# Hyena's engine order woven anew, and the odd filter spectra's sums formed in the attention stage

## The chip, the cores and the metric

One core of a Trainium2 chip runs the whole program. The metric is the device time in microseconds; lower is better. The engines are TensorE (PE, matrix products into PSUM), VectorE (DVE), ScalarE (ACT), GpSimd (POOL, which doesn't reach PSUM) and SyncE (SP, which here issues the weight loads). Each runs its own instruction stream in order and waits on counting semaphores.

## The reference

Two layers of a hybrid backbone run over 128 context and 512 latent tokens of width 1024. What bears on the change is the Hyena branch, `y = x0 * (h (*) (x1 * u) + bias * (x1 * u))`:

```python
def bidir_long_conv(u, h, bias):
    L, C = u.shape[1], u.shape[2]
    g = jnp.concatenate([h[:, 0], jnp.zeros((1, C), jnp.float32), h[:0:-1, 1]], axis=0)
    U = jnp.fft.rfft(u, n=2 * L, axis=1)
    G = jnp.fft.rfft(g, n=2 * L, axis=0)
    y = jnp.fft.irfft(U * G[None], n=2 * L, axis=1)[:, :L]
    return y + u * bias
```

`h` comes from a small sine MLP of the positions (`hyena_filters`), once per layer. Beside it a windowed attention runs on the same input projection. Each branch is projected, gated and merged, then comes a gated feed-forward part. The modulation of both groups of tokens is `silu(cond) @ w_ada + b_ada`.

## The kernel before

Features lie on the 128 partitions, the tokens of both groups along the row. Every f32 operand of a large product is split into a high and a low part (ACT writes `hi`, DVE writes `lo` = source - `hi`), and a product is three matmuls. Weights arrive in chunks of up to 1 MB in two raw buffers. SP issues them in the fixed order of `stream()`, and before item n it waits for the consumer of item n-2, so a load can't overtake the one ahead of it. Each chunk is split by `split(g)` on ACT and on DVE into one of two slots; a slot is free when the product of two chunks earlier has been made (`chunk_done`).

The Fourier transforms are matmuls with cosine and sine matrices, in five "pairs" of spectrum rows: pair 0 for the context, pairs 1 and 2 for the even frequencies of the latent tokens, pairs 3 and 4 for two parts of the odd ones.

**Prologue.** PE forms the filter rows of both layers (`filter_rows`, L545), DVE multiplies them by the window and forms sums and differences, five steps a layer (`filter_blocks`, L1559 to L1583), PE turns them into spectra (`g_spectrum`, L563), and ACT (later DVE) copies those out. POOL stores them to a DRAM buffer `g_kept` (`g_spill`). Before that `g_combine` (L2146, L2149) forms the sum and the difference of the odd pairs 3 and 4. In between, the first modulation vectors are made: chunks (0, 4) and (0, 5) of `w_ada` by PE (`ada`, L525), chunks (0, 6) and (0, 7) by DVE (`ada_t`, L1525). The stream's order is (0, 6), (0, 4), (0, 7), (0, 5), then the layer's weights. In the second layer's filter blocks `ada_t(0, 6)` stands behind step 1.

**Attention.** Five blocks; two tiles of the Hyena projection (z) lie beside each on PE. POOL is nearly idle.

**Hyena.** After the last block PE transposes u (`u_transposed`), then makes the last z tile, spectra 0 to 2 of u (`spectrum`, L797), four rows of the attention's projection (`attn_projected`, L781, which reads the chunk gA), the context's inverse (L942), spectra 3 and 4, and the latent inverses of pairs 1 to 4 (`inverse`, L819). The inverses read chunk gI, which lies in the slot of gA. DVE forms the complex products with the kept filter spectra (L1887 to L1905 for pairs 0 to 2, L1920 to L1939 for 3 and 4, which first add and subtract the two parts) and their low halves `y_lo` (L1631), and splits the chunks gA, gF1, gI and gG between them (L1618). ACT makes the high halves `y_hi`. Pairs 1 and 3, and 0, 2 and 4, share a slot of `y_hi` and `y_lo`. When the last `y_lo` is ready, POOL clears pads of `h_src_rows`, and ACT and DVE form the rows for the gates, of which PE's next tile takes one after the other (`both`, L691).

## Time and profile before

| | us |
|---|---|
| median of 3 runs (lowest, highest) | 2029.27 (2028.94, 2031.91) |
| profiled execution: time | 2029.84 |
| its span, first to last instruction | 2026.9 |
| PE busy | 1963.9 |
| DVE busy | 1168.8 |
| ACT busy | 740.6 |
| POOL busy | 195.6 |

Times in the views count from the span's start. The prologue lasts to about 97, the attention and Hyena stages of layer 0 to about 367, those of layer 1 from about 1060 to 1327. In a timeline row the number in brackets is the time that the engine stood idle before it, and what ended that. `x4` after the shapes is the number of instructions merged into the row.

### The profile page before, as it was taken

The page shows a single profiled execution, that of the slowest core. Times are in us where ns is not written, and L with a number is a line of the kernel's source. Part 1 is how long each engine was busy: PE and PEld are TensorE (multiplying, and loading weights), DVE is VectorE, ACT ScalarE, POOL GpSimd, SP SyncE. Part 2 cuts the span into 40 slices and gives each one's busy share as a digit, 9 for nine tenths or more (in the row PEclk, how much of TensorE's full clock was granted, in tenths as well). Part 3 has the DMA queues.
Part 4 walks back from the last instruction along what each step waited for, and adds up shares of the span by engine and source line. Part 5 has one row for each costly group of instructions (what it writes and reads, how often), then busy time and mean ns, then how long its engine had stood idle before and what let it go on. Part 6 is the DMA issues. An engine that isn't in the chain of part 4 may idle for free.

```text
span 2026.9 us, 30168 instructions
## 1 busy us (share of the span) xinstructions
PE 1963.9 (97%) x12914; PEld 1881.4 (93%) x12914; DVE 1168.8 (58%) x1743; ACT 740.6 (37%) x1098; POOL 195.6 (10%) x210
## 2 busy tenths in 40 slices
PE   8899998999999999999999999899999999999997
PEld 3599997999999999999989999899998999999996
DVE  7824559787477677767455456953347343243435
ACT  3534444422273321333244445532227332133313
POOL 0320001100150000000121000110015000000011
PEclk9999999999999999999999999899999999999999
DMA  8431012255213335443322101212221211221121
GB/s 329 154 116 66 16 56 99 99 189 185 85 63 128 143 141 196 153 166 120 106 73 100 48 27 61 84 60 92 78 79 63 84 63 65 91 84 63 64 72 53
DMA packets 37438, 203.39 MB, mean 100 GB/s; under 512 B 4294, under 2 KB 7927, under 8 KB 19256
## 3 DMA queue, kind: packets, MB, share of 16 engines
q1 hardware_dynamic: 30904, 181.37, 25.1%
q0 software_dynamic: 3312, 13.35, 1.9%
q10 hardware_dynamic: 3088, 6.75, 0.9%
q8 instruction: 101, 1.65, 0.3%
q14 instruction: 33, 0.27, 0.0%
HBM read 193.31 MB, written 8.14 MB: 99 GB/s over the span
## 4 chain that ended last, share of the span: by engine, by line
PE 83%; DVE 10%; ACT 4%; issue 2%; ACTq 0%; DMA 0%; POOL 0%; SPq 0%; DVEq 0%
PE gemm_psum L618 51%; PE gemm_psum L648 15%; PE gemm_psum L671 3%; PE gemm_psum L631 3%; PE aux_psum L758 2%; PE gemm_psum L691 2%; PE aux_psum L739 2%; PE aux_psum L747 1%; ACT h_src_rows L1186 1%; PE gemm_psum L525 1%; DVE aux_psum L1793 1%; PE gemm_psum L563 1%; DVE w_lo L1618 1%; DVE x L1797 1%; PE aux_psum L545 1%
## 5 line engine op out<-in xcount | busy, mean ns | idle before, releaser
L618 PE MATMUL gemm_psum<-h_hi,w_hi 128*128 128x322 f32 x2144 | 497.1, 313 | 0.3
L618 PE MATMUL gemm_psum<-h_hi,w_lo 128*128 128x322 f32 x2144 | 493.5, 311 | 0.0
L618 PE MATMUL gemm_psum<-h_lo,w_hi 128*128 128x322 f32 x2144 | 491.3, 310 | 0.0
L618 PEld LDWEIGHTS gemm_psum<-h_hi,w_hi 128*128 128x128 f32 x2144 | 362.8, 189 | 4.4 <-issue 3.1
L618 PEld LDWEIGHTS gemm_psum<-h_lo,w_hi 128*128 128x128 f32 x2144 | 362.1, 189 | 0.0
L618 PEld LDWEIGHTS gemm_psum<-h_hi,w_lo 128*128 128x128 f32 x2144 | 361.9, 189 | 0.0
L1618 DVE TENSOR_TENSOR w_lo<-w_raw,w_hi 128x2048 fp32r<-128x2048 f32 (+4 forms) x128 | 244.6, 1911 | 182.1 <-ACT w_hi L1116 181.1
L1116 ACT ACTIVATE w_hi<-w_raw 128x2048 fp32r<-128x2048 f32 (+4 forms) x128 | 204.1, 1594 | 170.7 <-PE gemm_psum L648 65.6
L1525 DVE CUSTOM_DVE_ANT_0 aux_psum<-w_raw,cond_by_row 128x1024 f32<-128x1024 f32 x160 | 191.0, 1257 | 5.0 <-DMA w_raw<-in_ada_t 4.7
L1751 DVE SCALAR_TENSOR_TENSOR x<-gemm_psum,mod,x 128x128 f32<-128x128 f32 (+2 forms) x144 | 55.4, 434 | 158.7 <-PE gemm_psum L648 128.9
L648 PE MATMUL gemm_psum<-act_hi,w_lo 128*128 128x322 f32 x616 | 141.9, 312 | 0.0
L648 PE MATMUL gemm_psum<-act_lo,w_hi 128*128 128x322 f32 x616 | 141.6, 311 | 0.0
L648 PE MATMUL gemm_psum<-act_hi,w_hi 128*128 128x322 f32 x616 | 141.5, 311 | 0.0
L1653 DVE SCALAR_TENSOR_TENSOR gate_acc<-gate_rows,par,gate_acc 128x642 f32<-128x642 f32 x88 | 80.2, 912 | 75.8 <-ACT gate_acc L1194 74.3
L1824 DVE TENSOR_TENSOR gate_acc<-gate_acc,gemm_psum 128x644 f32<-128x644 f32 x40 | 33.0, 826 | 143.7 <-PE gemm_psum L618 143.7
L648 PEld LDWEIGHTS gemm_psum<-act_hi,w_hi 128*128 128x128 f32 x616 | 104.3, 189 | 0.0
L648 PEld LDWEIGHTS gemm_psum<-act_hi,w_lo 128*128 128x128 f32 x616 | 104.2, 189 | 0.0
L648 PEld LDWEIGHTS gemm_psum<-act_lo,w_hi 128*128 128x128 f32 x616 | 103.9, 189 | 0.0
L1135 ACT ACTIVATE act_hi<-gate_acc 128x644 fp32r<-128x644 f32 x44 | 32.7, 742 | 153.5 <-DVE gate_acc L1824 147.1
L1193 ACT ACTIVATE gate_rows<-gemm_psum 128x644 f32<-128x644 f32 (+1 forms) x48 | 31.8, 662 | 144.4 <-PE gemm_psum L618 140.0
L2159 POOL TENSOR_TENSOR sums<-x 128x644 f32<-128x644 f32 x4 | 6.4, 1589 | 790.5 <-DVE x L1751 790.5
L671 PE MATMUL gemm_psum<-h_hi,w_hi 128*128 128x322 f32 x224 | 72.2, 323 | 10.3 <-POOL h_lo L2127 3.8
(349 smaller groups left out, 3264.5 us busy)
## 6 DMA issues: line engine op xcount, KB each, us to landing
w_raw<-in_w_up SPq DMA_DIRECT2D x44, 1024.0 KB, 4.8
w_raw<-in_ada_t SPq DMA_DIRECT2D x42, 1024.0 KB, 4.7
w_raw<-in_w_down SPq DMA_DIRECT2D x32, 704.0 KB, 4.1
w_raw<-in_w_gate SPq DMA_DIRECT2D x16, 1024.0 KB, 4.8
w_raw<-in_w_z SPq DMA_DIRECT2D x12, 1024.0 KB, 4.7
w_raw<-in_w_out SPq DMA_DIRECT2D x8, 1024.0 KB, 4.7
ada_early<-in_ada SPq DMA_DIRECT2D x4, 1024.0 KB, 19.4
g_kept<-g_rows_out POOLq DMA_DIRECT2D x8, 512.0 KB, 4.4
```

Of the source, the lines that this page charges most:

```text
L618: last = mm(gp[:, 2 * (t % 2) + hf, 0:HALF], w[:, off + P * kk:off + P * (kk + 1)], moving(kk, lo)[:, hf * HALF:(hf + 1) * HALF], start=kk ...
L631: last = mm(gp[:, 2 * (t % 2) + hf, 0:HALF], w[:, off + P * kk:off + P * (kk + 1)], moving(kk, lo)[:, half(hf)], start=kk == 0 and n == 0, ...
L648: last = mm(gp[:, 2 * (t % 2) + hf, 0:HALF], w[:, off + P * kk:off + P * (kk + 1)], moving(kk, lo)[:, half(hf)], start=kk == 0 and n == 0, ...
L671: last = mm(banks(c, p_, hf), w[:, P * (KD * c + kk):P * (KD * c + kk + 1)], (hlo if lo else hhi)[:, kk, half(hf)], start=kk == 0 and n == ...
L691: last = mm(gp[:, 2 * ((t0 + c) % 2) + hf, 0:HALF], w[:, P * (KD * c + kk):P * (KD * c + kk + 1)], moving(kk, lo)[:, hf * HALF:(hf + 1) * ...
L739: last = mm(ax[:, n % 4, at:at + P * m], q[pr, j, tok(b)], rhs, start=True, stop=True)
L758: last = mm(ax[:, 2, HD * n:HD * (n + 1)], p_t(n)[:, P * kb:P * (kb + 1)], v[:, HD * (n % 2):HD * (n % 2 + 1)], start=kb == 0, stop=kb == ...
L1116: run(whi[s][:, 0:n], raw[st_ % 2][:, 0:n], ACT.Copy).then_inc(sem["w_hi"], raised("w_hi"))
L1525: V.tensor_tensor_reduce(out=ada_out[:, :] if first else ax[:, 2 * gr:2 * gr + 2, :].rearrange("p a b -> p (a b)"), in0=raw[n % 2][:, D_MO ...
L1618: TT(wlo[s][:, 0:n], raw[STEP[(lane.layer, "g", g)] % 2][:, 0:n], f32(whi[s][:, 0:n]), ALU.subtract).then_inc(sem["w_split"], raised("w_sp ...
L1653: STT(acc[:, 1:ROW - 1], z[:, a:a + ROW - 2], w(tap), acc[:, 1:ROW - 1], ALU.mult, ALU.add).then_inc(sem[event if tap else "dve_order"], r ...
L1751: STT(x[:, m, a:b], gp[:, 2 * (t % 2) + h, a - HALF * h:b - HALF * h], mod[:, gate + m, gr:gr + 1], x[:, m, a:b], ALU.mult, ALU.add)\
```

## The change

- In the prologue `g_combine` is gone: all five pairs of both layers are stored as they come, and layer 1's four last stores stand between rows of `h_lo`. `ada_t(0, 6)` moves from behind step 1 to behind step 3.
- In each layer's attention stage POOL reads pairs 3 and 4 back into a new tile `g_parts` (in space that Hyena's `early` and `u_fold` use later), forms the sum and the difference in four operations and stores them over the old ones. DVE waits for these stores before it writes `u_fold`.
- In Hyena PE's order becomes: spectrum 0, last z tile, spectra 1 and 2, rows 0 and 1 of the projection, context inverse, row 2, spectra 3 and 4, row 3, inverses. The PSUM banks of the spectra and of row 2 move to suit.
- DVE's order becomes: products of pair 0 at once, then the u halves, gA's split, the x0 taps, low halves of pair 0, gF1's split, and so on; gI's split moves behind the first odd product, and the context's result ahead of the products of pair 2.
- The copies of one partition (`us[0:1]` from `prod[0:1]`) move from DVE to ACT. ACT makes the high halves of u's odd blocks (`u_hi(5, 9)`) later, and gI's split follows row 3 of the projection.

The diff, without the list of semaphores and with context lines cut (eight spaces of indentation taken off):

```diff
@@ -310,6 +310,8 @@
         ufold = sb("u_fold", [P, 4, HY_W], F32, s3)
+    with ExitStack() as s3:
+        g_parts = sb("g_odd_parts", [P, 5, HY_W], F32, s3)
     early = sb("attn_projected", [P, EARLY, ROW], F32, s2)
@@ -346,7 +348,6 @@
     feat = sb("feat", [FEAT, NT], F32, s2)
-g_first = sb("g_first_half", [P, 2, HY_W], F32, s)
 dreg = sb("d_block", [P, 2, HY_W], F32, s)
@@ -369,7 +370,7 @@
     ot_bank = lambda b: gp[:, 2, :] if b + 1 < NB else ax[:, 2, :]
-    spec_bank = lambda r: ax[:, r, :] if r < 2 else gp[:, r % 4, :]
+    spec_bank = lambda r: ax[:, r, :] if r < 2 else gp[:, (r - 2) % 4, :]
     ROPE_ORDER = [4, 0, 1, 2, 3]
@@ -430,7 +431,7 @@
     G_SLOT = [0, 1, 2, 0, 1]
-    EARLY_BANKS = [(1, 2), (1, 0), (1, 2), (1, 0)]
+    EARLY_BANKS = [(1, 2), (1, 0), (1, 0), (1, 0)]
@@ -911,29 +912,27 @@
     to_features(NB - 1)
-    pe.wait_ge(sem["at_lo"], due("at_lo", NB - 1))
-    tile(9, 1, KD, KD * P, h_mov, "z_mm")
-
     pe.wait_ge(sem["us_ready"], due("us_ready", 1))
...
     spectrum(0, U_V[0])
+    pe.wait_ge(sem["at_lo"], due("at_lo", NB - 1))
+    tile(9, 1, KD, KD * P, h_mov, "z_mm")
+
+    pe.wait_ge(sem["us_ready"], due("us_ready", 3))
+    spectrum(1, U_V[1])
     pe.wait_ge(sem["z_acc"], due("z_acc", 12))
-    for p_ in range(1, 3):
-        pe.wait_ge(sem["us_ready"], due("us_ready", 1 + 2 * p_))
-        spectrum(p_, U_V[p_])
+    pe.wait_ge(sem["us_ready"], due("us_ready", 5))
+    spectrum(2, U_V[2])
     pe.wait_ge(sem["w_split"], due("w_split", gA + 1))
...
     attn_projected(1)
-    for n in (2, 3):
-        pe.wait_ge(sem["pa_out"], due("pa_out", n - 1))
-        attn_projected(n)
...
     pe.wait_ge(sem["y_ready"], due("y_ready", 2))
-    pe.wait_ge(sem["pa_out"], due("pa_out", 3))
+    pe.wait_ge(sem["pa_out"], due("pa_out", 1))
     s = slot_of(gF1)
@@ -942,9 +941,13 @@
     last.then_inc(sem["cinv_mm"], raised("cinv_mm"))
+    pe.wait_ge(sem["pa_out"], due("pa_out", 2))
+    attn_projected(2)
     pe.wait_ge(sem["us_rest"], due("us_rest", 4))
...
     spectrum(4, U_V[4])
+    pe.wait_ge(sem["pa_out"], due("pa_out", 3))
+    attn_projected(3)
     pe.wait_ge(sem["w_split"], due("w_split", gI + 1))
@@ -1314,35 +1317,41 @@
     split(gA)
-    u_hi(5, 9)
...
+    def y_high(p_):
+
+        for o in range(2):
+            src = us[:, o, :] if p_ < 3 else (us, prod)[o][:, p_ - 3, :]
+            if p_ < 2:
+                act.wait_ge(sem["y_src"], due("y_src", 2 * p_ + o + 1))
+                run(us[0:1, o, :], prod[0:1, 1 - o, :], ACT.Copy).then_inc(sem["act_order"], raised("act_order"))
+                act.wait_ge(sem["act_order"], now("act_order"))
+            hi(yhi[:, Y_SLOT[p_], 1 - o, :], src, "y_src", 2 * p_ + o + 1, "y_hi")
+
     act.wait_ge(sem["usp_mm"], due("usp_mm", 4))
+    y_high(0)
     split(gF1)
-    for p_ in range(PAIRS):
-        for o in range(2):
-            if p_ == 2:
-                act.wait_ge(sem["cinv_mm"], due("cinv_mm", 1))
-            if p_ >= 3:
-                act.wait_ge(sem["linv_mm"], due("linv_mm", p_ - 2))
-            src = us[:, o, :] if p_ < 3 else (us, prod)[o][:, p_ - 3, :]
-            hi(yhi[:, Y_SLOT[p_], 1 - o, :], src, "y_src", 2 * p_ + o + 1, "y_hi")
-        if p_ == 0:
-            early_row(0)
-            early_row(1)
-        if p_ == 1:
-            early_row(2)
-            early_row(3)
-            split(gI)
-        if p_ == 2:
-            for o in range(2):
-                act.wait_ge(sem["usp_mm"], due("usp_mm", 7 + o))
-                run(ureg[:, 2 * o, :], spec_bank(6 + o), ACT.Copy).then_inc(sem["odd_out"], raised("odd_out"))
-            split(gG)
+    u_hi(5, 9)
+    early_row(0)
+    early_row(1)
+    y_high(1)
+    early_row(2)
+    for o in range(2):
+        act.wait_ge(sem["usp_mm"], due("usp_mm", 7 + o))
+        run(ureg[:, 2 * o, :], spec_bank(6 + o), ACT.Copy).then_inc(sem["odd_out"], raised("odd_out"))
+    act.wait_ge(sem["cinv_mm"], due("cinv_mm", 1))
+    y_high(2)
+    early_row(3)
+    split(gI)
+    split(gG)
+    for p_ in (3, 4):
+        act.wait_ge(sem["linv_mm"], due("linv_mm", p_ - 2))
+        y_high(p_)
     act.wait_ge(sem["usp_mm"], due("usp_mm", 10))
@@ -1569,7 +1578,7 @@
         TT(dreg[:, m % 2, :], fprod[:, 0, :], fprod[:, 1, :], ALU.subtract).then_inc(sem["gs_src"], 1)
-        if l and m == 1:
+        if l and m == 3:
             dve.wait_ge(sem["cond_rows"], 1)
@@ -1869,50 +1878,53 @@
     dve.wait_ge(sem["ut_out"], due("ut_out", 5))
+    dve.wait_ge(sem["g_kept_odd"], 48 * (L + 1))
     for n in range(4):
...
     u_lo(1, 3)
-    x0_tap(1, 0)
-    u_lo(3, 5)
-    x0_tap(1, 2)
-    split(gA)
-    for p_ in range(3):
+
+    def products(p_):
...
         ur, ui = spec_bank(2 * p_), spec_bank(2 * p_ + 1)
-        dve.wait_ge(sem[("g_first_in", "g_first_in", "g_mid_in", "g_odd_in", "g_last_in")[p_]], 16 * (L + 1))
+        dve.wait_ge(sem[("g_first_in", "g_first_in", "g_mid_in")[p_]], 16 * (L + 1))
+        if p_:
+            dve.wait_ge(sem["y_ready"], due("y_ready", 2 * p_))
         dve.wait_ge(sem["usp_mm"], due("usp_mm", 2 * p_ + 1))
         TT(prod[:, 0, :], ur, gr, ALU.mult).then_inc(sem["dve_order"], raised("dve_order"))
-        if p_:
-            dve.wait_ge(sem["y_ready"], due("y_ready", 2 * p_))
         TT(us[:, 0, :], ur, gi, ALU.mult).then_inc(sem["usp_out"], raised("usp_out"))
...
         dve.wait_ge(sem["dve_order"], now("dve_order"))
+        TT(us[:, 0, :], us[:, 0, :], us[:, 1, :], ALU.add).then_inc(sem["y_src"], raised("y_src"))
         dve.wait_ge(sem["usp_out"], now("usp_out"))
-        real = p_ < 2
-        TT(us[:, 0, :], us[:, 0, :], us[:, 1, :], ALU.add).then_inc(sem["dve_order" if real else "y_src"], raised("dve_order" if real else "y_src"))
-        if real:
-            dve.wait_ge(sem["dve_order"], now("dve_order"))
-            V.tensor_copy(us[0:1, 0, :], prod[0:1, 1, :]).then_inc(sem["y_src"], raised("y_src"))
         dve.wait_ge(sem["y_src"], now("y_src"))
-        TT(us[:, 1, :], prod[:, 0, :], prod[:, 1, :], ALU.subtract).then_inc(sem["dve_order" if real else "y_src"], raised("dve_order" if real else "y_src"))
-        if real:
-            dve.wait_ge(sem["dve_order"], now("dve_order"))
-            V.tensor_copy(us[0:1, 1, :], prod[0:1, 0, :]).then_inc(sem["y_src"], raised("y_src"))
+        TT(us[:, 1, :], prod[:, 0, :], prod[:, 1, :], ALU.subtract).then_inc(sem["y_src"], raised("y_src"))
+
+    def y_low(p_):
+
         for o in range(2):
-            ys = Y_SLOT[p_]
-            lo(ylo[:, ys, 1 - o, :], us[:, o, :], yhi[:, ys, 1 - o, :], "y_hi", 2 * p_ + o + 1, "y_ready")
-        if p_ == 0:
-            split(gF1)
-    split(gI)
+            src = us[:, o, :] if p_ < 3 else (us, prod)[o][:, p_ - 3, :]
+            lo(ylo[:, Y_SLOT[p_], 1 - o, :], src, yhi[:, Y_SLOT[p_], 1 - o, :], "y_hi", 2 * p_ + o + 1, "y_ready")
+
+    products(0)
+    u_lo(3, 5)
+    split(gA)
+    x0_tap(1, 0)
+    x0_tap(1, 2)
+    y_low(0)
+    split(gF1)
+    products(1)
+    y_low(1)
     dve.wait_ge(sem["cinv_mm"], due("cinv_mm", 1))
...
                ALU.mult, ALU.add).then_inc(sem["cinv_out" if j == 3 else "dve_order"], raised("cinv_out" if j == 3 else "dve_order"))
+    products(2)
+    y_low(2)
     for o in range(2):
@@ -1933,14 +1945,14 @@
         TT(ui, us[:, 0, :], us[:, 1, :], ALU.add).then_inc(sem["dve_order"], raised("dve_order"))
+        if at == 0:
+            split(gI)
     dve.wait_ge(sem["dve_order"], now("dve_order"))
...
     for p_ in (3, 4):
-        for o in range(2):
-            lo(ylo[:, Y_SLOT[p_], 1 - o, :], (us, prod)[o][:, p_ - 3, :], yhi[:, Y_SLOT[p_], 1 - o, :],
-               "y_hi", 2 * p_ + o + 1, "y_ready")
+        y_low(p_)
     split(gG)
@@ -2133,21 +2145,21 @@
         pool.wait_ge(sem["gsp_out"], 10 * l + 2 * n + 2)
-    pool.dma_start(g_kept[l, :, GSP_PAIRS[n]], g_first[:, :] if n == 1 else gst[:, GSP_PAIRS[n]]).then_inc(sem["g_spill"], 16)
+    pool.dma_start(g_kept[l, :, GSP_PAIRS[n]], gst[:, GSP_PAIRS[n]]).then_inc(sem["g_spill"], 16)
...
-    if l:
-        pool.wait_ge(sem["g_spill"], 16 * PAIRS)
-    if l:
-        pool.wait_ge(sem["gsp_late"], 2)
-    pool.wait_ge(sem["gsp_out"], 10 * l + (4 if l else 6))
+    pool.dma_start(g_parts[:, 0:4], g_kept[l, :, 3:5].rearrange("p a b c -> p (a b) c")).then_inc(sem["g_parts_in"], 16)
+    pool.wait_ge(sem["g_parts_in"], 16 * (l + 1))
     for o in range(2):
-        G.tensor_tensor(g_first[:, o, :], gst[:, 3, o, :], gst[:, 4, o, :], ALU.add).then_inc(sem["g_halves"], 1)
-    pool.wait_ge(sem["g_halves"], 4 * l + 2)
-    for o in range(2):
-        G.tensor_tensor(gst[:, 4, o, :], gst[:, 3, o, :], gst[:, 4, o, :], ALU.subtract).then_inc(sem["g_halves"], 1)
-    pool.wait_ge(sem["g_halves"], 4 * l + 4)
+        whole = g_parts[:, 4 if o == 0 else 0, :]
+        G.tensor_tensor(whole, g_parts[:, o, :], g_parts[:, 2 + o, :], ALU.add).then_inc(sem["g_halves"], 1)
+        pool.wait_ge(sem["g_halves"], 4 * l + 2 * o + 1)
+        G.tensor_tensor(g_parts[:, 2 + o, :], g_parts[:, o, :], g_parts[:, 2 + o, :], ALU.subtract)\
+            .then_inc(sem["g_halves"], 1)
+        pool.wait_ge(sem["g_halves"], 4 * l + 2 * o + 2)
+        pool.dma_start(g_kept[l, :, 3, o], whole).then_inc(sem["g_kept_odd"], 16)
+    pool.dma_start(g_kept[l, :, 4], g_parts[:, 2:4]).then_inc(sem["g_kept_odd"], 16)
@@ -2179,11 +2189,8 @@
                 h_lo(0, h, d)
-                if d == KD - 1:
-                    if h:
-                        g_combine(1)
-                    for n in (1, 2) if h else (3, 4):
-                        g_spill(1, n)
+                if h == 0 and d in (3, 5, 6, 7):
+                    g_spill(1, (1, 2, 3, 4)[(3, 5, 6, 7).index(d)])
     pool.wait_ge(sem["h_ready"], due("h_ready", 2 * KD))
@@ -2192,6 +2199,10 @@
     pool.wait_ge(sem["kv_dma"], 32 * (L + 1))
+    if L == 0:
+        pool.wait_ge(sem["g_spill"], 16 * PAIRS * DEPTH)
+    g_combine(L)
+    pool.wait_ge(sem["g_kept_odd"], 48 * (L + 1))
     pool.wait_ge(sem["pv_mm"], due("pv_mm", 40))
```

## Rows read from the trace of the kernel before

**Rows 1.** The page, part 1: busy us of each engine, its share of the span, instructions.
```profile
PE 1963.9 (97%) x12914; PEld 1881.4 (93%) x12914; DVE 1168.8 (58%) x1743; ACT 740.6 (37%) x1098; POOL 195.6 (10%) x210
```

**Rows 2.** TensorE's waits, both Hyena stages: us in total, times, longest us.
```profile
PE aux_psum L819 <- DVE y_lo L1631: 8.0, 1, 8.0
...
PE aux_psum L819 <- DVE y_lo L1631: 8.1, 1, 8.1
```

**Rows 3.** Timeline of POOL, prologue: start us, us, what, [idle before, releaser].
```profile
53.76 3.39 POOL L2146 TENSOR_TENSOR g_first_half<-g_rows_out 128x512 f32<-128x512 f32 x2 [19.71 <-ACT g_rows_out L1068]
...
57.23 4.33 POOL L2149 TENSOR_TENSOR g_rows_out<-g_rows_out 128x512 f32<-128x512 f32 x2
```

**Rows 4.** Timeline of DVE, prologue.
```profile
54.26 1.75 DVE L1571 TENSOR_TENSOR d_block<-filter_prod 128x512 f32<-128x512 f32 x1
...
55.94 2.29 DVE L1525 CUSTOM_DVE_ANT_0 ada_products<-w_raw,cond_by_row 128x1024 f32<-128x1024 f32 x1
...
63.83 1.28 DVE L1559 TENSOR_TENSOR filter_prod<-aux_psum,windows 128x512 f32<-128x512 f32 x2
...
66.95 1.29 DVE L1559 TENSOR_TENSOR filter_prod<-aux_psum,windows 128x512 f32<-128x512 f32 x2
...
74.48 1.22 DVE L1525 CUSTOM_DVE_ANT_0 ada_products<-w_raw,cond_by_row 128x1024 f32<-128x1024 f32 x1
...
81.87 0.17 DVE L1509 SCALAR_TENSOR_TENSOR mod<-gemm_psum,par 128x16 f32<-128x16 f32 x1 [1.16 <-PE gemm_psum L599]
```

**Rows 5.** Timeline of PE, prologue.
```profile
56.40 3.60 PE L525 MATMUL gemm_psum<-w_raw,cs 128*2 128x512 f32 x8
...
64.57 3.78 PE L545 MATMUL aux_psum<-w,h2T 128*128 128x512 f32 x4 [4.57 <-DVE filter_prod L1559]
...
74.31 3.59 PE L525 MATMUL gemm_psum<-w_raw,cs 128*2 128x512 f32 x8
```

**Rows 6.** Timeline of SyncE's queue, prologue.
```profile
64.31 0.65 SPq L500 DMA_DIRECT2D w_raw<-in_ada  x1
```

**Rows 7.** DMA issues in 60 to 70: KB each, median us to landing.
```profile
w_raw<-in_ada SPq DMA_DIRECT2D x1, 1024.0 KB, 8.1
```

**Rows 8.** One-us window: busy us of each engine, PEclk (granted clock), DMA share, GB/s.
```profile
68.00:69.00 1.00, 1.00 (x4) 0.72 (x3) 1.00 (x3) 0.00 (x0) 0.00 (x0) 0.56 0.92 377
```

**Rows 9.** Timeline of DVE, attention, block 0 of layer 0.
```profile
176.96 0.29 DVE L1717 COPY p_t<-aux_psum 128x128 f32<-128x128 f32 x1 [6.41 <-PE aux_psum L747]
```

**Rows 10.** Timeline of ACT, Hyena, layer 0.
```profile
290.69 1.08 ACT L1297 ACTIVATE u_blocks<-aux_psum 128x512 f32<-128x512 f32 x2
...
320.65 1.91 ACT L1116 ACTIVATE w_hi<-w_raw 128x2048 fp32r<-128x2048 f32 x1
```

**Rows 11.** Chain of waits in order of time, Hyena, layer 0: start us, us, what.
```profile
290.16 7.17 PE gemm_psum L618 x48
```

**Rows 12.** Timeline of DVE, Hyena, layer 0.
```profile
306.52 1.77 DVE L1897 TENSOR_TENSOR u_spec<-u_spec 128x512 f32<-128x512 f32 x1
...
310.49 0.41 DVE L1905 COPY u_spec<-prod 1x512 f32<-1x512 f32 x1
...
325.19 2.29 DVE L1618 TENSOR_TENSOR w_lo<-w_raw,w_hi 128x2048 fp32r<-128x2048 f32 x1
...
328.43 0.68 DVE L1920 TENSOR_TENSOR u_blocks<-u_blocks,gemm_psum 128x512 f32<-128x512 f32 x1
...
343.20 0.69 DVE L1631 TENSOR_TENSOR y_lo<-prod,y_hi 128x512 fp32r<-128x512 f32 x1
```

**Rows 13.** Timeline of POOL, Hyena, layer 0.
```profile
303.77 5.69 POOL L2202 TENSOR_TENSOR v_lo<-u_blocks,v_hi 128x512 fp32r<-128x512 f32 x4
```

**Rows 14.** Two-us windows of both Hyena stages, columns as in rows 8.
```profile
338.00:340.00 2.00, 0.00 (x0) 0.00 (x0) 1.97 (x4) 0.23 (x1) 0.00 (x0) 0.63 0.00 0
...
344.00:346.00 2.00, 2.00 (x13) 2.00 (x13) 2.00 (x1) 1.75 (x3) 0.12 (x3) 0.66 0.00 0
...
1306.00:1308.00 2.00, 2.00 (x12) 2.00 (x11) 1.35 (x3) 1.97 (x4) 0.65 (x1) 0.52 0.51 123
```

More of the change, by code:

```diff
@@ L231, in _program @@
               "w3_in", "w3_next_in", "ada_in0", "ada_in1", "ada_in2", "ada_in3", "win_first_in", "win_rest_in", "pre_hi", "pre_split", "filt_mm", "filt_out", "filt_order",
-              "gs_src", "g_halves", "gs_hi", "gs_ready", "gsp_mm", "gsp_out", "g_spill", "g_first_in", "g_mid_in", "g_odd_in", "g_last_in",
+              "gs_src", "g_parts_in", "g_halves", "g_kept_odd", "gs_hi", "gs_ready", "gsp_mm", "gsp_out", "g_spill", "g_first_in", "g_mid_in", "g_odd_in", "g_last_in",
               "cond_ready", "mod_next", "aff_ffn", "aff_next", "x_norm", "ident_in", "mlp_mm", "mlp_arg", "mlp_sin", "mlp_order", "mask_done",
@@ L2172, in _ @@
                 for n in range(PAIRS):
-                    if n == 1:
-                        g_combine(0)
                     g_spill(0, n)
```

## The prediction

> **What bounds the kernel now.** I read the page's busy line first: TensorE (PE) is busy for 1963.9 of 2026.9 us [rows 1], so nothing but its idle time and its slow-clock time can move. PE's waits, taken over the two stretches that the diff touches, come next: in each layer's Hyena stage one wait, of 8.0 and of 8.1 us, is for VectorE's (DVE's) low halves of the last spectrum products [rows 2]. The timelines of the engines in those stretches then say what DVE is doing meanwhile. The prologue is the third place: there PE waits 4.57 us for DVE's filter products and then runs slowly [rows 5]. The reader is to see that both places are chains over several engines, so that an edit counts only by what it does to the last link.
>
> **The prologue (filter spectra, before layer 0).** Removed: g_combine(0), four GpSimd (POOL) operations from 53.76 to 61.56 [rows 3]. They are not on the chain, but DVE's work beside them is stretched: its difference block takes 1.75 us, and four modulation reductions (L1525) run from 55.94 to 63.91, the first at 2.29 us, where a later one takes 1.22 and four take 4.94 (74.48 to 79.42) [rows 4]. Without the combine DVE has back 1.06 + 3.03 = 4.1 us.
> The Trainium skill, "SBUF — State Buffer", on the port pair that VectorE and GpSimd share, says that a VectorE instruction with two SBUF inputs and a GpSimd one that reads SBUF exclude each other for a whole instruction; the trace agrees, with the 2.29 us above. By that rule alone the prologue would be shorter, which is the second rival below.
> Moved: ada_t(0, 6), from behind filter step 1 to behind step 3. Step 1 now ends at 54.26 + 0.69 = 54.95. A step takes 3.12 us (the one that ends at 66.95 began at 63.83, where the reductions end) [rows 4], so steps 2 and 3 end at 61.2 and the reductions at 61.2 + 4.94 = 66.15, against 63.91 before: 2.2 us later, in spite of the 4.1 saved. PE gains: its filter rows 8 and 9 no longer wait. ada(4) ends at 59.95 [rows 5], the two rows take 1.9 at full clock (half of the 3.78 shown), the two spectra 5.6, so PE stands before ada(5) at 67.4 instead of 74.31 [rows 5].
> What is late next is the weight load. SyncE's queue runs in order: the load of chunk (0, 7) waits for those reductions, and ada(5)'s chunk is behind it. Before, it was issued at 64.31 [rows 6] and landed 8.1 us later [rows 7], at 72.4. Now it is issued at about 66.6. Four transfers shared the DMA engines before (two chunks, two 0.5 MB spills), about three do now; between 7.0 and 8.1 us I take 7.4: it lands at 74.0. PE has idled 6.6 us by then. After the 4.57 us of idle time before, the granted clock was at its lower level, 1.2 GHz, until about 68.5 (mean 0.56 in 68 to 69 [rows 8]), 3.9 us after work began again. The same 3.9 us at half speed cost ada(5) 1.95 us: it ends at 74.0 + 3.53 + 1.95 = 79.5 against 77.84. The first modulation follows at 83.5 instead of 81.87 [rows 4], and everything up to the first projection follows it, over ScalarE (ACT). Term: **+1.6 us**. Bounds: if the load takes 7.0 us and the clock stays high, -0.7; if it takes 8.1 and the lower clock lasts over ada(5) and the next spectrum (3.5 + 2.8 us of full-clock work, doubled), +6.5 with the 0.3 of a later start. I stay by the middle, since the ramp has a row.
> ada_t(0, 7)'s chunk, one place ahead, lands near 72.5, so its reductions end at 77.5, before PE's transposes: hidden. The spills of layer 1, four POOL issues of about 0.55 us moved between h_lo rows, and the combine of layer 1 taken out from behind them: PE starts the first projection on DVE's w_lo and eats one h row in 0.9 us, so a row that is 1 us late is covered. Zero; two late rows, should they open it, are 1 us.
>
> **The attention stage.** Added on POOL per layer: one 1 MB load, four tensor operations, three stores, from about 157 on, when POOL is idle until 288. The price of one operation is bounded by 1.42 us (a quarter of the four v_lo operations [rows 13]) and 2.17 (half of the 4.33 of two sums beside DVE's reductions [rows 3]); I take 1.4, since the v_lo ones too run beside plain DVE work. They can block DVE, whose conv and w_lo run there: 4 x 1.42 = 5.7 us. The cover is DVE's idle time of 6.41 us ahead of 176.96 [rows 9]. Zero; without the cover, or at the upper bound (8.7 us), it would be up to 2.3 us a layer in the way of p_t. DVE's new wait on g_kept_odd is met 100 us ahead of its turn; behind it stand the u_fold sums and everything in Hyena. Reading the sums back is what it was.
>
> **Hyena, layer 0.** (1) PE now runs spectrum 0 before the last z tile. It needs the last u block, copied by ACT at 290.69 + 1.08 = 291.77 [rows 10]; the tile started at 290.16 and ran 7.17 [rows 11]. So PE idles 1.6 us, spectrum 0 (2.8) runs to 294.6, the tile to 301.8, 4.5 us later than before. (2) DVE forms products(0) in the time in which it waited for that tile; but ACT still has the z rows ahead of u_hi(3,5), so those halves arrive at 304.4 and DVE idles 4.6 us after products(0), and 1.1 more for w_hi of gA. Spectrum 2 ends at 308.0 instead of 305.5. (3) The four one-partition copies leave DVE; each costs it 0.41 us where POOL does not block it [rows 12], 1.6 us in all. They go to ACT, at 0.5 to 0.6 each, with slack except before y_high(1). (4) POOL's four v_lo operations (5.69 us [rows 13]) now come at 310 to 319, beside y_low, gF1's split and products(1). As before two of them should fall on PSUM-fed products and two block DVE: the sum at 306.52 took 1.77 instead of 0.69 [rows 12]. They cancel. (5) pa3 (3.6 us) moves behind the spectra 3 and 4, which therefore end at 327.7 (gA's low half is ready at 308.5, then pa0 and pa1 7.2, cinv 2.7, pa2 3.6, the spectra 5.7): DVE's odd sums, which wait for them (328.43 before [rows 12]), are done at 329.9 instead of 331.1. Gain 1.2 us.
> (6) The loss: split(gI) writes the weight slot that pa3 reads. Before, its low half (2.29 us at 325.19 [rows 12]) lay on DVE under the spectra. Now pa3 ends at 331.2, ACT copies row 3 (0.7) and makes the high half (1.91 [rows 10]) until 333.8, and DVE makes the low half at 333.8 to 336.1 in the middle of the odd products: +2.3 on the chain. Low halves of pair 3 begin 1.0 us later than before. (7) PE idles from 331.2 to 336.1, 4.9 us, and only then starts the inverses of pairs 1 and 2, which lay under DVE before. Their 48 matmuls, 5.7 us at full clock (342.1 less 8.0 less 328.4), end at 341.8. In the old gap, which opened at 334.1 (342.1 less the 8.0 of waiting), the clock fell after 4.4 us (0.63 in 338 to 340) and came back 3.3 us after work resumed in layer 0, 5.3 in layer 1 (0.66 and 0.52 [rows 14]). So it falls here too, and the inverses end at 343.5 (344.5). y_high(4) waits for pair 2's inverse, so the last y_low, at 343.20 + 0.69 = 343.9 before [rows 12], ends at 345.6 (346.7); 345.0 if the clock stays. From it hang POOL's pads, ACT's h rows, DVE's h_lo and PE's first gate tile, an unchanged chain. Terms: **+1.8 us in layer 0, +2.8 in layer 1**; each between -0.5 (the POOL block vanishes and ACT's waits with it) and +3.5 (four POOL operations block instead of two).
>
> **Sum.** 1.6 + 1.8 + 2.8 = +6.2 us. The profiled execution took 2029.84 us (span 2026.9 and 2.9 around it), 0.6 above the median of 2029.27: 2036.0 on it, **2035.5 us** on the median.
>
> **Rivals.** (B) Faster: the freed DVE decides the prologue. If ada(5)'s chunk lands by 69, PE does not wait; then the first modulation is set by DVE: chunk (0, 7) at 70.9, reductions 4.94, one filter block 1.3, so 77.1, a gain of 4.7 us. With Hyena's PE gap of 8 us turned into work at no loss, 2029.3 - 4.7 = 2024.6. For it: the 4.57 us wait is real and goes. Against: a landing in under 3 us, when the shown one took 8.1. It decides only below about 70. Chance 0.12. (C) The clock does not fall in the three new gaps and the terms are -0.3, +1.1 and +1.1: 2031.2 us, no measurable change. For it: gaps of 4.9 us are only just longer than the 4.4 after which it fell. Chance 0.30. (D) The clock stays low over ada(5) and the spectrum, and four POOL operations block: 6.5 + 2 x 3 = +12.5, 2041.8 us. [...] Chance 0.10.
>
> **How the numbers follow.** The forecast has 0.48, with its own range 2032 to 2039. About 0.2% (4 us) is what a measurement of this kernel tells from no change. Faster: B, 0.12. Same: C and the low end of the forecast, 0.34. Slower: 0.54. The range 2026 to 2040 leaves out B and half of D.
>
> **What would show it.** In the profile after: the reductions at L1525 at 1.22 us each and ending near 66; ada(5) on w_raw after a PE wait for a DMA of over 5 us; the first modulation near 83.5; in Hyena PE idle 1.6 us before the first spectrum, and 4.9 before the inverse with DVE's w_lo as releaser, in place of the single wait of 8.0; the last y_low near 345.5. The prediction is wrong if the first modulation comes before 81, or if the last y_low comes before 343.9: then the wait for the load, or the wait for split(gI), is not the link that I take it for.

## The result, and the profile after

The changed kernel takes 2040.2 us (median of 5, 2038.3 to 2040.4), the kernel before 2029.1: ratio 1.0046, 95% interval 1.0035 to 1.0057. That is slower, as forecast, but by 9.3 us and not by 6.2: 2038.6 on the earlier median, at the upper end of the forecast's own range. The medians of these runs lie 11.1 us apart and their means 9.6; the new median itself lies 0.2 us above the range of 2026 to 2040. All times and ratios here are of executions in the fast state, and hyena_alone and combine_alone are read by their times alone, since their profiled executions ran at a mean granted clock of 0.39 and 0.85.

The page of the profile after, its first lines, and TensorE's waits in the prologue, in Hyena of layer 0 and of layer 1 (columns: us in total, times, longest):

```profile
span 2038.4 us, 30180 instructions
...
PE 1971.0 (97%) x12914; PEld 1884.5 (92%) x12914; DVE 1170.0 (57%) x1735; ACT 745.2 (37%) x1106; POOL 202.8 (10%) x218
```

```profile
PE gemm_psum L526 <- DMA w_raw<-in_ada: 6.9, 1, 6.9
PE gemm_psum L564 <- ACT g_rows_out L1071: 2.2, 1, 2.2
...
PE aux_psum L820 <- DVE w_lo L1627: 4.9, 1, 4.9
PE gemm_psum L692 <- DVE h_lo L1640: 2.2, 2, 1.7
PE aux_psum L798 <- ACT u_blocks L1300: 1.8, 1, 1.8
...
PE gemm_psum L798 <- DVE v_lo L1640: 0.7, 1, 0.7
...
PE gemm_psum L692 <- DVE h_lo L1640: 3.2, 5, 1.7
```

The single wait of 8 us of [rows 2] is gone. In its place stand 4.9 us for the low half of the inverse weights and 1.8 us ahead of spectrum 0, and the prologue has a new wait of 6.9 us for the weights of ada(5), chunk (0, 5) of `w_ada`. TensorE's busy time grew by 7.1 us against [rows 1], though its work is the same. Most of that is matmuls at the lower clock: half of TensorE's busy time in the low stretches is 12.5 us, before 6.8 (an estimate from the windows).

The prologue after, from the timelines of VectorE, SyncE and TensorE (start, duration, engine and line, tiles; idle time before it):

```profile
61.47 1.22 DVE L1534 CUSTOM_DVE_ANT_0 ada_products<-w_raw,cond_by_row 128x1024 f32<-128x1024 f32 x1
...
65.27 1.23 DVE L1534 CUSTOM_DVE_ANT_0 ada_products<-w_raw,cond_by_row 128x1024 f32<-128x1024 f32 x1
...
66.53 0.33 SPq L501 DMA_DIRECT2D w_raw<-in_ada_t  x1
66.91 0.46 SPq L501 DMA_DIRECT2D w_raw<-in_ada  x1
...
74.77 5.99 PE L526 MATMUL gemm_psum<-w_raw,cs 128*2 128x512 f32 x8 [6.88 <-DMA w_raw<-in_ada]
...
84.72 0.17 DVE L1518 SCALAR_TENSOR_TENSOR mod<-gemm_psum,par 128x16 f32<-128x16 f32 x1 [6.33 <-PE gemm_psum L600]
```

With the combine gone the reductions of [rows 4] take 1.22 us each, yet they end at 66.5, and the load behind them lands 7.8 us after its issue. The first modulation comes 2.85 us later than in [rows 4].

Layer 0's Hyena stage after: the odd sums, the split of the inverse weights, the last high and low halves:

```profile
331.67 0.68 DVE L1932 TENSOR_TENSOR u_blocks<-u_blocks,gemm_psum 128x512 f32<-128x512 f32 x1
...
338.20 2.29 DVE L1627 TENSOR_TENSOR w_lo<-w_raw,w_hi 128x2048 fp32r<-128x2048 f32 x1
...
348.88 0.63 ACT L1138 ACTIVATE y_hi<-u_spec 128x512 fp32r<-128x512 f32 x1 [1.67 <-PE aux_psum L820]
...
350.16 0.69 DVE L1640 TENSOR_TENSOR y_lo<-prod,y_hi 128x512 fp32r<-128x512 f32 x1
```

Hyena began 3.96 us later than before (the first u block was copied at 291.88, before at 287.92). Less that, the odd sums begin 0.7 us earlier than in [rows 12] and the last low half 3.0 us later.

Following the same instructions through both timelines gives the whole account of the 11.5 us between the two spans:

| stretch | offset after it, us | cost |
|---|---|---|
| start to the first modulation | 2.85 | 2.85 (of it 0.3 at the very start) |
| to the first u block of layer 0 | 3.96 | 1.1 |
| Hyena, layer 0 | 6.93 | 3.0 |
| to the first u block of layer 1 | 7.53 | 0.6 |
| Hyena, layer 1 | 10.16 | 2.6 |
| to the last output | 11.57 | 1.4 |

The attention stage costs nothing: the offset is 4.0 at the first projection and 3.96 at its end. Inside it VectorE does run late beside POOL's four operations. The same four z operations, before and after, and the copy behind them, which had 6.41 us of idle time ahead of it in [rows 9]:

```profile
162.53 3.40 DVE L1653 SCALAR_TENSOR_TENSOR z_acc<-z_rows,par,z_acc 128x642 f32<-128x642 f32 x4
```

```profile
167.49 6.75 DVE L1662 SCALAR_TENSOR_TENSOR z_acc<-z_rows,par,z_acc 128x642 f32<-128x642 f32 x4
...
180.93 0.29 DVE L1726 COPY p_t<-aux_psum 128x128 f32<-128x128 f32 x1 [3.15 <-PE aux_psum L748]
```

The idle time took up the delay, and 3.15 us of it are left.

Three of the stretches in the table hold work that was not touched (1.1, 0.6 and 1.4 us). For two of them the granted clock of one-microsecond windows says why (columns: length, busy us of PE, PEld, DVE, ACT, POOL with their instructions, PEclk, DMA share, GB/s). The row at 79 belongs to ada(5), those at 340 to 345 to the inverses in Hyena of layer 0:

```profile
79.00:80.00 1.00, 1.00 (x3) 0.20 (x2) 0.00 (x0) 0.00 (x0) 0.00 (x0) 0.69 0.99 418
...
88.00:89.00 1.00, 0.00 (x0) 0.00 (x0) 0.96 (x2) 0.97 (x3) 0.23 (x1) 1.00 0.00 0
...
92.00:93.00 1.00, 1.00 (x4) 0.71 (x3) 0.74 (x4) 0.97 (x4) 0.00 (x0) 0.50 0.00 0
94.00:95.00 1.00, 1.00 (x6) 0.79 (x5) 0.54 (x1) 0.97 (x4) 0.98 (x3) 1.00 0.07 16
...
340.00:341.00 1.00, 0.45 (x2) 0.45 (x3) 1.00 (x2) 0.00 (x0) 0.00 (x0) 0.50 0.00 0
344.00:345.00 1.00, 1.00 (x7) 1.00 (x7) 0.97 (x3) 0.00 (x0) 0.00 (x0) 0.50 0.00 0
345.00:346.00 1.00, 1.00 (x7) 1.00 (x7) 1.00 (x2) 0.00 (x0) 0.00 (x0) 0.57 0.00 0
...
2020.00:2021.00 1.00, 0.00 (x0) 0.00 (x0) 1.00 (x4) 0.45 (x2) 0.00 (x0) 1.00 0.57 205
2022.00:2023.00 1.00, 1.00 (x3) 0.61 (x2) 0.98 (x3) 1.00 (x3) 0.00 (x0) 0.50 0.50 173
```

Near 90 and near 2022 TensorE ran at 1.2 GHz after an idle time of only 2.2 and 2.0 us. The kernel before has the same two idle times, and in its profile the clock stayed at 2.4 GHz through both (its timeline and windows):

```profile
86.98 0.47 PE L563 MATMUL gemm_psum<-filter_hi,w_hi 128*128 128x512 f32 x1 [2.22 <-ACT g_rows_out L1068]
...
2011.27 0.78 PE L829 MATMUL aux_psum<-sums,ones 128*128 128x322 f32 x2 [1.98 <-DVE x L1751]
...
88.00:89.00 1.00, 0.63 (x3) 0.19 (x1) 0.28 (x1) 1.00 (x3) 0.75 (x1) 1.00 0.36 143
2012.00:2013.00 1.00, 0.97 (x4) 0.38 (x3) 0.72 (x2) 1.00 (x3) 0.00 (x0) 1.00 0.34 115
```

### The profile page after: what moved, and what is told of

It is laid out like the page before. It is cut to its first block, busy times and chain, and to the rows that moved or that the text cites. A ratio compares the mean times of both kernels' runs of the same rounds, so it can differ in the third digit from the quotient of the medians.

```text
span 2038.4 us, 30180 instructions
## 1 busy us (share of the span) xinstructions
PE 1971.0 (97%) x12914; PEld 1884.5 (92%) x12914; DVE 1170.0 (57%) x1735; ACT 745.2 (37%) x1106; POOL 202.8 (10%) x218
## 3 DMA queue, kind: packets, MB, share of 16 engines
q10 hardware_dynamic: 3088, 6.75, 0.9%
q8 instruction: 101, 1.65, 0.3%
## 4 chain that ended last, share of the span: by engine, by line
PE 82%; DVE 9%; ACT 4%; DMA 2%; issue 2%; ACTq 0%; SPq 0%; POOL 0%; DVEq 0%
PE gemm_psum L619 51%; PE gemm_psum L649 11%; PE gemm_psum L672 3%; PE gemm_psum L632 3%; PE aux_psum L759 2%; DMA w_raw<-in_ada_t 2%; PE gemm_psum L692 2%; DVE aux_psum L1534 2%; PE aux_psum L740 2%; PE aux_psum L748 1%; PE aux_psum L782 1%; ACT h_src_rows L1189 1%; PE gemm_psum L526 1%; DVE w_lo L1627 1%; PE gemm_psum L564 1%
## 5 line engine op out<-in xcount | busy, mean ns | idle before, releaser
L1534 DVE CUSTOM_DVE_ANT_0 aux_psum<-w_raw,cond_by_row 128x1024 f32<-128x1024 f32 x160 | 191.0, 1258 | 13.5 <-DMA w_raw<-in_ada_t 13.2
```

The costliest lines, as they stand in the source:

```text
L1534: V.tensor_tensor_reduce(out=ada_out[:, :] if first else ax[:, 2 * gr:2 * gr + 2, :].rearrange("p a b -> p (a b)"), in0=raw[n % 2][:, D_MO ...
```

## The experiments

Two theories stood at the start. T: the loss has two independent places, the order of SyncE's loads in the prologue, and Hyena's chain with the late split of the inverse weights and the clock in the gap before them. R: the stages hang together, over the moved combine or over DMA traffic. All ratios are to the kernel before, and the differences in us are worked out from them; most have an interval of 2 us to either side. In the edits shown, waits are left out.

**hyena_alone**

All of Hyena's new order on the kernel before, with its prologue and its combine; the first of the edits:

```
+            spectrum(0, U_V[0])
             tile(9, 1, KD, KD * P, h_mov, "z_mm")
...
```

> The kernel before with the new engine order of Hyena alone; the prologue and the combine stay as they were. Theory (the loss has two independent places): the two Hyena stages carry +3.0 and +2.65 us in the profile after, so +5.7: 2034.8 us, ratio 1.0028. In the profile PE idles 4.9 us before the first inverse in both layers, for DVE's low half of the inverse weights, and the first modulation stays at 81.9. Rival (the stages hang together: Hyena only loses because the prologue shifted it, or because of the combine's loads in the attention stage): no loss here, 2029.1. Second rival (three further falls of the clock that the profile after shows, at 89, 362 and 2021 us, are the effect of the new Hyena order): more than +7.

Measured: 2036.7 us, 1.0035 (1.0022 to 1.0049), +7.1 (4.5 to 9.9). Hyena loses by itself, so the first rival falls. The interval holds both the theory's +5.7 and the second rival. The later profiles speak against that one: load_swapped and warm_combine, with Hyena's old order, show falls of the clock in the prologue and at the end too.

**prologue_alone**

The rest of the change without Hyena: g_combine in the attention stage, and

```
-                if l and m == 1:
+                if l and m == 3:
```

> The kernel before with everything of the change but Hyena's order: the combine in the attention stage and ada_t(0, 6) behind filter step 3. Theory: first modulation at 84.7 (before 81.9), first projection 4.0 us later than before, nothing in the attention stage: +4.0, 2033.1 us, ratio 1.0020; with the fall of the clock at the end of the kernel too it is +5.3. Rival (the combine on POOL costs time in the attention stage, up to 2.3 us a layer, and the two parts share one cause): +7 and more.

Measured: 2032.0 us, 1.0011 (1.0002 to 1.0019), +2.2. First modulation at 83.55, 1.7 us later than before and not 2.85; the first u block 1.65 later, so again nothing in the attention stage. That is less than the expected +4.0: here the clock stayed up near 90, and it came back 3.3 us into ada(5) where the profile after has 4.9. The two parts add: 0.35% and 0.11% are the 0.46% of the whole change.

**combine_alone**

On prologue_alone:

```
-                if l and m == 3:
+                if l and m == 1:
```

> As the run before, but ada_t(0, 6) stays behind filter step 1: only the combine is moved. Theory (the order on DVE decides when SyncE issues the load of ada(5)): reductions 55.0 to 59.9, loads issued near 60.5, landed near 68, filter steps 2 and 3 end at 66.2, PE before ada(5) near 70 with no wait for a DMA, first modulation near 77.9: -4.0 us against before, 2025.1 us, ratio 0.9980. Rival (the load was late for DMA traffic, not for its issue): the wait for the load stays over 4 us, and the time is within 1 us of the kernel before, 2029. Second rival (POOL's combine in the attention stage blocks DVE): 2030 and more.

Measured: 2027.5 us, 0.9989 (0.9980 to 0.9998), -2.2. Moving the combine is a gain; ada_t(0, 6) turned it into a loss. The gain is about half of the expected 4.0. In warm_combine, which has the same prologue, the first modulation comes at 79.30 and not near 77.9, and 1.1 us of the 2.6 gained are lost where the clock fell near 86.

**ada_t_back**

The same edit on the kernel after.

> The kernel after with ada_t(0, 6) back behind filter step 1, all else as changed. Theory: the prologue turns from +4.0 to -4.0 while Hyena keeps its +5.7: 2040.2 - 8.0 = 2032.2, ratio to the kernel before 1.0008 to 1.0020. If the parts add, this run less the kernel before equals the runs hyena_alone and combine_alone together. Rival (the load is late for DMA traffic): 2039 to 2040.

Measured: 2034.9 us, 1.0023 (1.0013 to 1.0032), -4.7 against after where -8.0 was expected. The parts add again (0.35 less 0.11 is 0.24). The wait for the load is gone, the first modulation comes at 79.28, and then 1.1 us of the 2.6 gained are lost near 86, where the clock fell in this profile too.

**load_swapped**

On prologue_alone:

```
-        for n, (L, what, i) in enumerate(STREAM):
+        for n in (0, 1, 2, 3, 5, 4) + tuple(range(6, len(STREAM))):
+            L, what, i = STREAM[n]
```

> The run prologue_alone (ratio 1.0011) with one edit: SyncE issues the load of ada(5)'s chunk ahead of that of chunk (0, 7), whose slot comes free only after the reductions of ada_t(0, 6). Theory (the wait of 6.8 us for that load is the place in SyncE's in-order queue and nothing else): it is issued near 60 instead of 66.9, TensorE's wait before ada(5) is under 1 us, ada(5) takes 3.6 us at full clock, and the first modulation comes at 79.3 (83.55 there, 81.87 before), set now by chunk 7's reductions: -4.2 us, ratio 0.9991. Rival (the load is late for the traffic of the spills): the wait stays over 4 us and the ratio at 1.0011.

Measured: 2027.5 us, 0.9987 (0.9978 to 0.9995), -4.9 against prologue_alone. SyncE's timeline, ada(5) on TensorE with no wait and the load's time from issue to landing, here and then in prologue_alone:

```profile
59.92 0.33 SPq L502 DMA_DIRECT2D w_raw<-in_ada  x1
66.05 0.33 SPq L502 DMA_DIRECT2D w_raw<-in_ada_t  x1
...
67.35 3.59 PE L527 MATMUL gemm_psum<-w_raw,cs 128*2 128x512 f32 x8
...
82.84 0.77 PE L565 MATMUL gemm_psum<-filter_hi,w_hi 128*128 128x512 f32 x1 [5.04 <-ACT g_rows_out L1070]
...
w_raw<-in_ada SPq DMA_DIRECT2D x1, 1024.0 KB, 4.7
```

```profile
74.38 5.22 PE L526 MATMUL gemm_psum<-w_raw,cs 128*2 128x512 f32 x8 [6.78 <-DMA w_raw<-in_ada]
...
w_raw<-in_ada SPq DMA_DIRECT2D x1, 1024.0 KB, 7.7
```

The first modulation comes at 77.74. So the place in the in-order queue decides: with the load issued 6.7 us earlier the whole wait is gone, and the rival falls. Other transfers were not free, though. Issued ahead of its neighbour the load landed after 4.7 us, issued right behind it after 7.7; so an estimate is that 3 us of the old wait came from sharing the DMA engines. TensorE now waits 5.04 us ahead of the last spectra, the clock is low from 81 to 88, and 1.6 us of the earlier modulation are lost by the first projection.

**gi_back** and **tile_first**, both on ada_t_back

gi_back, with split(gI) also put ahead of the copies of spectrum 3 on ACT and of the odd sums on DVE:

```
             attn_projected(2)
+            attn_projected(3)
             spectrum(3, U_V[3])
             spectrum(4, U_V[4])
-            attn_projected(3)
```

> The run ada_t_back with attn_projected(3) and the split of the inverse weights put back ahead of spectra 3 and 4 and of the odd products. Theory A (the split in the middle of the odd products, +2.3 us, is what the new order loses): -2 to -3 us a layer, so -4 to -6: ratio 0.9995 to 1.0003. Theory B (in the new order TensorE is late too: its idle time ahead of the tile puts the end of spectrum 4 3.6 us later once attn_projected(3) stands before it, and VectorE's odd sums with it): +2.9 us a layer, +5.8: ratio 1.0052. A hand schedule from the durations of the rows says B.

tile_first:

```
-            spectrum(0, U_V[0])
             tile(9, 1, KD, KD * P, h_mov, "z_mm")
+            spectrum(0, U_V[0])
```

> The run ada_t_back (+4.7 us against the kernel before) with one edit: TensorE runs the last z tile before spectrum 0 again, all other orders stay the new ones. Theory (part of Hyena's loss is TensorE's 1.8 us of idle time ahead of spectrum 0, which moves the tile, the last x0c row and all that VectorE does behind it): the last low half of each layer comes 1.6 us earlier, so -3.3 us: +1.4 against before, ratio 1.0007. Rival (the whole loss hangs on the late split of the inverse weights): no change against ada_t_back, 1.0023.

Measured: gi_back 2040.5 us, 1.0049 (1.0035 to 1.0062); tile_first 2028.9 us, 0.9993 (0.9984 to 1.0002). To take the split out of the odd products makes it worse by 5 us, to put the z tile back in its place makes it better by 6, where 3.3 was expected. The two profiles of tile_first and ada_t_back put 4.8 us of that into the Hyena stages and 1.0 into the prologue, where the clock did not fall near 68 this time. In Hyena a part is POOL's: its v_lo operations now block one VectorE operation, the second below at 1.61 us, and no longer the low halves and the split, which took 1.1 us more each in the new order:

```profile
306.55 1.49 DVE L1627 TENSOR_TENSOR w_lo<-w_raw,w_hi 128x1280 fp32r<-128x1280 f32 x1
...
311.14 1.61 DVE L1905 TENSOR_TENSOR u_spec<-prod 128x512 f32<-128x512 f32 x1
```

TensorE's waits in gi_back in layer 0, the end of its spectrum 4, and VectorE around the split:

```profile
PE aux_psum L820 <- DVE y_lo L1640: 6.1, 1, 6.1
PE aux_psum L820 <- DVE w_lo L1627: 2.0, 1, 2.0
...
329.69 0.39 PE L798 MATMUL gemm_psum<-v_hi,w_lo 128*128 128x512 f32 x1
...
328.55 1.29 DVE L1640 TENSOR_TENSOR y_lo<-u_spec,y_hi 128x512 fp32r<-128x512 f32 x2 [4.84 <-ACT y_hi L1138]
329.77 2.28 DVE L1627 TENSOR_TENSOR w_lo<-w_raw,w_hi 128x2048 fp32r<-128x2048 f32 x1
331.97 0.68 DVE L1933 TENSOR_TENSOR u_blocks<-u_blocks,gemm_psum 128x512 f32<-128x512 f32 x1
```

Spectrum 4 ends 44.8 us after the first u block (copied at 285.25), against 40.2 in ada_t_back (326.65 less 286.46): theory B's delay, 4.6 where 3.6 was expected. But the run has a cost of its own too: VectorE waits 4.84 us for y_high(2), the high halves of pair 2, which in this ACT order stand behind row 3, the split and the copies of spectrum 3. Were they made ahead of row 3, the low halves and the split would end at about 329.3 and the first sum start 2.7 us earlier, which is most of the 2.8 to 3.1 us that the stage lost. So an estimate for undoing the split alone is an even result, no gain; it was not run, and no run moved the split with the z tile in front. The table below takes Hyena by its length, from the copy of the first u block on ACT to the first hy_lo on DVE:

| profile | layer 0, us | layer 1, us |
|---|---|---|
| before | 76.87 | 76.89 |
| after | 79.84 | 79.52 |
| ada_t_back | 80.24 | 80.03 |
| gi_back | 83.06 | 83.09 |
| tile_first | 77.14 | 78.29 |
| warm_after | 78.25 | 78.25 |
| warm_combine | 76.81 | 76.82 |
| tile_warm | 76.35 | 76.37 |

**warm_after**, on ada_t_back

```
             attn_projected(3)
+            pe.wait_ge(sem["odd_out"], due("odd_out", 2))
+            for n in range(18):
+                mm(gp[:, 0, :], ath[:, 0, 0:P], ath[:, 0, 0:HY_W], start=True, stop=True)
             pe.wait_ge(sem["w_split"], due("w_split", gI + 1))
```

> The run ada_t_back with 18 matmuls of 128x512 added on TensorE in its 4.9 us of idle time before the first inverse, into a bank that nobody reads (4.2 us at full clock); the results are as before. Theory (the fall of the clock in that gap makes the inverses of pairs 1 and 2 take 8.4 us instead of 5.7, and pair 2's inverse holds back the last high halves by 1.5 us): granted clock 1.0 from 335 to 345, the last low half 1.5 us earlier in each layer, -3 us against ada_t_back: ratio 1.0008. Rival (the slow clock lies beside VectorE's odd products and costs nothing): 1.0023.

Measured: 2030.5 us, 1.0001 (0.9992 to 1.0010), -4.5 against ada_t_back. The windows of the stage, and y_high(4) on ACT, which waited 1.67 us for pair 2's inverse in the profile after:

```profile
336.00:337.00 1.00, 1.00 (x11) 1.00 (x11) 1.00 (x3) 0.00 (x0) 0.00 (x0) 1.00 0.60 172
340.00:341.00 1.00, 1.00 (x10) 0.91 (x8) 1.00 (x3) 0.93 (x2) 0.00 (x0) 1.00 0.00 0
...
341.15 0.63 ACT L1141 ACTIVATE y_hi<-u_spec 128x512 fp32r<-128x512 f32 x1 [0.23 <-PE aux_psum L820]
```

So 1.8 to 2.0 us a layer were the slow clock's (80.24 and 80.03 against 78.25), and 1.4 us the order's (78.25 against 76.87). The clock's share is more than the expected 1.5 us a layer.

**warm_combine**, on combine_alone: 30 such matmuls between the inverses of pairs 2 and 3

> The run combine_alone (-2.2 us against the kernel before; Hyena as before) with 30 matmuls of 128x512 added on TensorE in the old gap of 8.0 us between the inverses of pairs 2 and 3, 7.0 us at full clock. Theory (the clock falls in that gap, and the inverses of pairs 3 and 4 run for 3.2 us in layer 0 and 5.3 in layer 1 at 1.2 GHz, on the chain to the gate tiles): -1.6 and -2.6 us, so -6.4 in all against before: ratio 0.9968. Rival (the gate tile waits for the h rows anyway, so faster inverses are not seen): 0.9989.

Measured: 2027.4 us, 0.9987 (0.9978 to 0.9995), no more than combine_alone. The clock fell in the old gap too [rows 14], but behind it stood only the gate tile, which waits for h rows: the rival was right, and a fall of the clock in the kernel before cost Hyena no more than 0.06 to 0.07 us a layer.

**tile_warm** (tile_first with the 18 matmuls), **tile_warm_swapped** and **tile_warm_ends**, the last with

```
             for pair_ in GSP_PAIRS[1:]:
+                if pair_ == 4:
+                    pe.wait_ge(sem["filt_out"], 20)
+                    for n in range(8):
+                        mm(ax[:, 0, :], whi[PRE_SLOT[1]][:, 0:P], ...)
...
+        for n in range(7):
+            mm(ax[:, 3, :], whi[0][:, 0:P], whi[0][:, 0:HY_W], start=True, stop=True)
         ln_stats(1, 1, due)
```

> The run tile_first (0.9993) with the 18 idle matmuls of the run warm_after in the gap before the first inverse. There the stage from the first u block to the first hy_lo took 77.14 us in layer 0, where the clock fell for 3.4 us, and 78.29 in layer 1, where it fell for 6.8. Theory (both parts add): 76.5 us in both layers, against 76.9 in the kernel before, -2.4 against tile_first: ratio 0.9981. Rival (without the slow clock the next limit is VectorE's odd products, which tile_first already reached): 77.1 in both, ratio 0.9987.

> The run tile_warm with ada_t(0, 6) behind filter step 3, as in the change, and the two loads swapped as in load_swapped. Theory: the first modulation at 79.3, no later than with ada_t behind step 1 (78.2 to 79.3), and TensorE has no idle time before the filter rows 8 and 9 at which the clock fell near 68: within 1 us of tile_warm, 0.9976 to 0.9986. Rival (TensorE waits for the load all the same): +3.5 us against tile_warm, 0.9998.

> The run tile_warm with idle matmuls on TensorE at two more places, 8 before the spectra of the fourth pair in the prologue (2.2 us of idle time near 85, where the clock fell in five of the profiles so far) and 7 before the last sums of squares (2.0 us of idle time at the end, where it fell in some). Theory (each fall costs the 1.1 to 1.3 us that the offsets between the profiles show there): -1.1 to -2.4 against tile_warm, ratio 0.9970 to 0.9976. Rival (the falls lie beside other work or do not come in most executions): 0.9981.

Measured: tile_warm 2027.3 us, 0.9987 (0.9978 to 0.9996); tile_warm_swapped 2026.3 us, 0.9981 (0.9972 to 0.9990); tile_warm_ends 2023.8 us, 0.9969 (0.9958 to 0.9981). The stage of tile_warm is 76.4 us as expected, but its total misses by 1.2 us and is the rival's. The falls near 84 and at the end don't explain that, for tile_first has them too. The profiles put 1.0 us of it between the Hyena stages (884.1 against 883.1 us), where neither differs in its program, and the cause is open. tile_warm_swapped came as expected: the loads' order is worth as much as ada_t's place. With idle matmuls in those two gaps as well the kernel is the fastest of all, 6.3 us under the kernel before and 3.7 under tile_warm, more than the 2.4 expected at most. Of the 3.3 us between the two profiled spans the two gaps have 2.4, and 0.8 lie between the Hyena stages again. Near 85 in tile_warm, then in tile_warm_ends:

```profile
84.00:86.00 2.00, 2.00 (x5) 1.10 (x5) 1.25 (x4) 2.00 (x5) 0.88 (x1) 0.50 0.15 61
```

```profile
84.00:86.00 2.00, 1.41 (x7) 0.84 (x6) 1.13 (x4) 2.00 (x5) 0.88 (x1) 1.00 0.22 90
```

## Why the prediction was right in sign and short in size

**Prologue, +1.6.** Right in mechanism and, for this part alone, in size: prologue_alone has its first modulation 1.7 us later, and 2.2 us in all. The links came as told in the profile after: reductions 1.22 us each to 66.5 (66.15), a wait of 6.9 us (6.6) for a load issued at 66.9, ada(5) 5.99 us (5.5). What the clock costs was read wrongly. At two levels, a mean of 0.56 in 68 to 69 [rows 8] is a low clock for 0.88 of that window, so it came back near 68.9, 4.3 us after work resumed and not 3.9. In the same way the 0.69 in 79 to 80 gives 4.9 us after, and prologue_alone's profile 3.3. The whole change's profile has 2.3 us more there than prologue_alone's: 1.2 up to the first modulation, of which 0.8 is that longer low clock over ada(5), and 1.1 for the fall near 90, for which the prediction had no step.

**Attention, 0.** Right in both layers, and by the cover that was named: the idle time ahead of p_t fell from 6.41 to 3.15 us in layer 0.

**Hyena, +1.8 and +2.8.** Measured 3.0 and 2.6. By warm_after 1.4 us of each is the order (the prediction's "if the clock stays" was 1.1), the rest the clock. The steps came true one by one: idle 1.8 us ahead of spectrum 0 (1.6), odd sums earlier by 0.7 (1.2), TensorE idle 4.9 (4.9), the low half of the inverse weights done at 336.5 on the old time axis (336.1), the last low half at 346.9 in layer 0 (345.6). The missing 1.3 us there are mostly the clock: it came back 5.3 us after TensorE resumed at 340.55, where 3.3 had been taken from the kernel before; in layer 1 it was 4.5 where 5.3 had been taken. Neither sign of being wrong came, the first modulation before 81 or the last low half before 343.9. Low halves on DVE beside the four v_lo of POOL took 2.40 us for two and 2.60, where 1.46 and 1.49 stood before; the old overlap had cost the sum and the copy beside it as much, so step (4), "they cancel", holds.

**What failed is the attribution in step (6), "The loss".** The late split does lie on the chain, but the runs show no gain from undoing it: in gi_back spectrum 4 ends 4.6 us later, more than the 2.3 us of the split, and the stage is 3 us longer (about even, by the estimate above, without that run's own wait). The order's loss was made in steps (1) and (2), by spectrum 0 ahead of the z tile. With the slow clock taken out of both, the tile's place is worth 1.9 us a layer (78.25 in warm_after, 76.35 in tile_warm), and with the tile first this order, late split and all, beats the old one by 0.5 us a layer. Whether an early split would then gain more is open. The prediction counted steps (1) and (2) as idle times of 1.6 and 4.6 us and did not ask what the stage would be without them; and it took POOL's block (4) as the same in any order, though tile_first has 1.3 us less of it.

**The size.** The profiled spans lie 11.5 us apart, 5.3 more than the forecast. Of that 1.25 came before the first modulation (0.3 at the very start, 0.5 more until the load had landed, at 74.8 and not 74.0, and 0.5 by the clock), 1.1 near 90, 1.2 in layer 0 of Hyena, 0.6 between the Hyena stages and 1.4 at the end, 1.3 of it the fall there; layer 1 took 0.2 less. Between the stages VectorE waits 13.2 us for the loads of ada_t, 4.7 before; whether that is the 0.6 no run tests. The two falls of the clock at 2 us gaps, 2.4 us in this profile, come in some executions and not in others, so part of the distance from the forecast is chance, and so is part of any closeness.

**The rivals.** Rival C had the clock not fall; it fell in six places (low from 72, 89, 339, 362, 1301 and 2021) where the prediction had counted three. Rival D is near in number (2041.8) but not in kind: over ada(5) the clock was back at 79.6, before the spectrum, and POOL's v_lo cost VectorE no more than before. Rival B, the freed DVE, is real once the load is out of its way: load_swapped has the first modulation at 77.7, where B had put it at 77.1.

## What to carry to other kernels

When a step is moved on one engine, look up which in-order queue waits for its result, and what stands behind that wait: here one load, 6.8 us. A visible wait need not be the loss: the late split was what TensorE waited for, and the place of the z tile, which showed 1.8 us of waiting, was worth more: 1.9 us a layer. An idle time of TensorE of 2 us can cost a fall of its clock. Where a bank and an operand are free, idle matmuls in the gap took that out and cost nothing that these runs show, but only a gap with a chain behind it paid.
